# Hyena and short-convolution projections as seven block products per quad, on one Trainium2 core

## What is computed

```python
p = h @ lp['w_in']                       # h (2048, 1024)
yb = hyena_branch(p[..., B_OFF:C_OFF], lp, rows)    # 768 columns
yc = shortconv_branch(p[..., C_OFF:G_OFF], lp, rows) # 768 columns
# hyena: u = short_conv(pb, hy_conv_w, rows) + hy_conv_b
#        x0, x1, v = split(u, 3); z = x1 * v; y = x0 * (longconv(z) + z * hy_d_bias)
# shortconv: bg, cg, hx = split(pc, 3); y = bg * short_conv(cg * hx, sc_conv_w, rows)
# short_conv: three taps along each row of 64 tokens, zero at the row ends
```

## Time and profile before

| | us |
|---|---|
| runs of the kernel before, median (lowest to highest of 3) | 4469.63 (4462.31 to 4470.07) |
| the profiled execution | 4470.81 |
| its span in the profile | 4469.0 |
| projection stage, first to last matmul | 1412.43 to 1755.34 |
| gates' stage, first matmul | 2192.33 |

### The profile page before, as it was taken

One profiled execution on the slowest core, in us unless ns is written; L12 is line 12 of the kernel. 1 busy time (PEld: TensorE's weight loads), 2 busy tenths in 40 slices (PEclk: granted clock), 3 DMA queues, 4 the chain that ended last, 5 costly groups with the idle time before them and its releaser, 6 DMA issues. The chain is left out here.

```text
span 4469.0 us, 42953 instructions
## 1 busy us (share of the span) xinstructions
PE 3992.4 (89%) x15090; PEld 2435.5 (54%) x15090; DVE 1362.0 (30%) x2515; ACT 864.7 (19%) x1729; POOL 676.2 (15%) x536
## 2 busy tenths in 40 slices
PE   6999988989898998784499999989958999999994
PEld 2444445888886443242244444435537777777773
DVE  4433324666664121413322232212141111111112
ACT  4444441223222110020111111111100000000002
POOL 1122112333331000011100111112211000000000
PEclk9999998999999999897699999999969999999997
DMA  6333321222121101543311111124342455445544
GB/s 250 117 97 104 97 58 66 71 70 70 67 69 48 29 9 37 172 141 123 115 47 52 56 47 59 47 94 154 122 171 96 147 191 207 156 159 202 198 143 176
DMA packets 293866, 484.19 MB, mean 108 GB/s; under 512 B 20939, under 2 KB 171150, under 8 KB 293510
## 3 DMA queue, kind: packets, MB, share of 16 engines
q1 hardware_dynamic: 269618, 417.47, 27.0%
q0 software_dynamic: 12096, 43.86, 3.8%
q10 hardware_dynamic: 12053, 21.56, 1.5%
HBM read 372.05 MB, written 110.77 MB: 108 GB/s over the span
## 5 line engine op out<-in xcount | busy, mean ns | idle before, releaser
L2460 PE MATMUL bank<-xeT,wgu 128*128 128x256 f32 x3072 | 667.2, 380 | 9.9 <-PE bank L2474 9.8
L2460 PEld LDWEIGHTS bank<-xeT,wgu 128*128 128x128 f32 x3072 | 582.4, 190 | 100.9 <-issue 22.1
L627 PE MATMUL bank<-hT,wq 128*128 128x512 f32 x1024 | 450.1, 593 | 0.0
L1335 PE MATMUL bank<-hT,wh 128*128 128x512 f32 x768 | 336.5, 598 | 12.6 <-DMA wh<-in_w_in 9.6
L2474 PE MATMUL bank<-wd,hid_e 128*128 128x512 f32 x768 | 332.3, 592 | 1.5 <-DVE hid_e L2381 1.5
L627 PEld LDWEIGHTS bank<-hT,wq 128*128 128x128 f32 x1024 | 192.5, 190 | 224.9 <-issue 224.3
L1853 PE MATMUL bank<-hT,raw_w 128*128 128x512 f32 x576 | 261.1, 596 | 6.5 <-DMA raw_w<-in_w_in 6.5
L1335 PEld LDWEIGHTS bank<-hT,wh 128*128 128x128 f32 x768 | 145.6, 191 | 197.1 <-issue 197.1
L2111 PE MATMUL bank<-wo,mt 128*128 128x512 f32 x512 | 227.8, 599 | 15.7 <-DMA wo<-in_w_out 15.7
L2474 PEld LDWEIGHTS bank<-wd,hid_e 128*128 128x128 f32 x768 | 144.7, 190 | 177.9 <-issue 177.9
L2379 DVE TENSOR_TENSOR gm<-sgm,bank 128x256 f32<-128x256 f32 x96 | 40.4, 421 | 602.2 <-ACT sgm L2402 602.2
(11 more groups left out here) (351 smaller groups left out, 5223.7 us busy)
## 6 DMA issues: line engine op xcount, KB each, us to landing
wgu<-in_exp_w_gate SPq DMA_DIRECT2D x16, 3072.0 KB, 22.8
wgu<-in_exp_w_up SPq DMA_DIRECT2D x16, 3072.0 KB, 29.8
wd<-in_exp_w_down SPq DMA_DIRECT2D x16, 3072.0 KB, 13.5
ada<-in_ada_w SPq DMA_DIRECT2D x12, 2048.0 KB, 9.8
raw_w<-in_w_in SPq DMA_DIRECT2D x24, 1024.0 KB, 5.2
fa_d<-az ACTq DMA_DIRECT2D x48, 264.0 KB
sp_in<-fa_d SPq DMA_DIRECT2D x66, 192.0 KB, 4.1
kT<-kT_d SPq DMA_DIRECT2D x36, 256.0 KB, 2.8
```

What stands on the lines that cost most here:

```text
L627: last = pe.matmul(PS[g % 4][:, 0:width(n)], wq[:, kind, k, :], h_of(k, toff(n), width(n)), start=(k == 0), stop=(k == KD - 1))
L1335: last = pe.matmul(PS[u % 4][:, :], wh[:, kind, k, :], h_of(k, toff(n + 1), TW), start=(k == 0), stop=(k == KD - 1))
L2460: last = pe.matmul(PS[4 + f % 2][:, g * CAP:(g + 1) * CAP], wgu[:, b, g, k, f * P:(f + 1) * P], xeT[:, b, k, :], start=(k == 0), stop=(k = ...
```

## The change

The projection stage is rewritten with the gates' scheme. The unit is now a quad: one kind (256 columns, both halves) by 1024 tokens; 12 quads, 6 kinds for each half of the tokens. A quad is 7 products of 4 matmuls: p1, p5, c11, u2, c12, u3, c21. So 12 x 28 = 336 matmuls. Banks 0 and 1 take turns as X, banks 2 and 3 are Y and Z. VectorE gets four weight sums for each quad, four token sums for each half of the tokens, and three result sums for each quad. T3 has a tile of its own, since `hT` is read again by the gates' stage. Taps and products follow block by block (`middle` on ScalarE, `post` and `product_of` on VectorE). z is now made in `zT` itself, which gets its own memory; the GpSimd copy is gone. `yaT` is allocated later, and in the gates' stage T1 and T2 lie in the memory of `zT`, which is dead by then. The stage is unrolled, the store of z is issued by SyncE, and a load brings 1 MB for each quad. Nothing else is changed.

The core of the diff, indented less (the helpers `w`, `t`, `product`, `kept`, `s1` to `s4`, `t1`, `t2` and `t4` are as in the gates' stage):

```diff
@@ -1293,147 +1293,321 @@
-yaT = sbt(yst, "yaT", [P, HEADS, SEQ])
-zT = yaT[:, 0:2, :]
+zT = sbt(yst, "zT", [P, 2, SEQ])
...
+    T1, T2, T3, T4 = [sbt(st, n, [P, 4, TW]) for n in ("T1_h", "T2_h", "T3_h", "T4_h")]
+    p1s, p5s, u2s = [sbt(st, n, [P, TW]) for n in ("p1s_h", "p5s_h", "u2s_h")]
+    cb, cs = sbt(st, "cb_h", [P, 3, TW]), sbt(st, "cs", [P, 4, TW])
+    tmp, tm2, nat = [sbt(st, n, [P, 2, TW]) for n in ("tmp_h", "tm2", "nat_h")]
+    quads = [(p, kind) for p in range(2) for kind in range(6)]
+    NQ, QP = 12, 6
+    places = [(0, 0), (0, 1), (1, 1), (1, 0)]
+    conv_kinds = (0, 1, 2, 5)
+    convs = lambda q, i: sum(4 for v in quads[:q] if v[1] in conv_kinds) + i + 1
...
+    X, Y, Z = lambda q: PS[q % 2], PS[2], PS[3]
+    def at(v, q, i):
+        h, c = places[i]
+        return v[:, h, (2 * quads[q][0] + c) * TW:(2 * quads[q][0] + c + 1) * TW]
+    def summand(q, i):
+        kind = quads[q][1]
+        if kind == 3:
+            return at(ycT, q, i)
+        if kind == 4:
+            return cs[:, i, :]
+        return X(q)[:, :] if i == 3 else cb[:, i, :]
...
+            load_raw(0)
+            load_raw(1)
+            for q in range(1, NQ + 1):
+                p, kind = quads[q - 1]
+                if q + 1 < NQ:
+                    sp.wait_ge(c21_mm, q)
+                    load_raw(q + 1)
+                if kind == 3:
+                    for i, (h, c) in enumerate(places):
+                        sp.wait_ge(znat_ok, turned(p, i))
+                        sp.dma_start(z_d[(2 * p + c) * TW:(2 * p + c + 1) * TW, h * P:(h + 1) * P].rearrange("(j p) c -> p j c", p=P),
+                                     nat[:, i % 2, :].rearrange("p (j c) -> p j c", c=P)).then_inc(z_st[i % 2], 16)
+            for b in range(2):
+                sp.wait_ge(z_st[b], 64)
...
+            def turn(q, i):
+                p = quads[q][0]
+                pe.wait_ge(post_ok, convs(q - 1, i))
+                if turned(p, i) > 2:
+                    pe.wait_ge(znat_ok, turned(p, i) - 2)
                 for j in range(4):
+                    last = pe.transpose(PS[4 + i % 2][:, j * P:(j + 1) * P], at(zT, q, i)[:, j * P:(j + 1) * P], eye[:, :])
                 last.then_inc(z_tr, 1)
+            for q in range(NQ):
+                p, kind = quads[q]
+                pe.wait_ge(raw_in[q % 2], 16 * (q // 2 + 1))
+                if q >= 2:
+                    pe.wait_ge(x_free, q - 1)
+                product(X(q), w(q, 0, 0), t(p, 0, 0), True).then_inc(p1_mm, 1)
+                pe.wait_ge(s1_ok, q + 1)
+                pe.wait_ge(t1_ok, p + 1)
+                if q >= 1:
+                    pe.wait_ge(c12_ok, q)
+                product(Z, S1, T1, True).then_inc(p5_mm, 1)
+                if q >= 1:
+                    pe.wait_ge(c11_ok, q)
+                product(Y, w(q, 0, 1), t(p, 1, 0), True).then_inc(c11_mm, 1)
+                if kind == 3:
+                    turn(q, 0)
+                pe.wait_ge(s2_ok, q + 1)
+                pe.wait_ge(t2_ok, p + 1)
+                pe.wait_ge(p1s_ok, q + 1)
+                product(X(q), S2, T2, False).then_inc(u2_mm, 1)
+                if kind == 3:
+                    turn(q, 1)
+                pe.wait_ge(s4_ok, q + 1)
+                pe.wait_ge(p5s_ok, q + 1)
+                product(Z, S4, t(p, 1, 1), False).then_inc(c12_mm, 1)
+                if kind == 3:
+                    turn(q, 2)
+                pe.wait_ge(s3_ok, q + 1)
+                pe.wait_ge(t3_ok, p + 1)
+                pe.wait_ge(u2s_ok, q + 1)
+                product(X(q), w(q, 1, 0), T3, False).then_inc(u3_mm, 1)
+                if kind == 3:
+                    turn(q, 3)
+                pe.wait_ge(t4_ok, p + 1)
+                pe.wait_ge(c22_ok, q + 1)
+                product(X(q), w(q, 1, 1), T4, False).then_inc(c21_mm, 1)
...
+            for q in range(NQ):
+                if q >= 1:
+                    middle(q - 1, 3)
+                kept(p1s, X(q), p1_mm, c11_ok, p1s_ok, q)
+                kept(p5s, Z, p5_mm, c22_ok, p5s_ok, q)
+                middle(q, 0)
+                to_nat(q, 0)
+                kept(u2s, X(q), u2_mm, c12_ok, u2s_ok, q)
+                middle(q, 1)
+                to_nat(q, 1)
+                to_nat(q, 2)
+                middle(q, 2)
+                to_nat(q, 3)
+            middle(NQ - 1, 3)
...
+            def summed(q, i, bank, mm, other, other_ok, ok):
+                dve.wait_ge(mm, q + 1)
+                dve.wait_ge(other_ok, q + 1)
+                if q >= 1 and quads[q - 1][1] in conv_kinds:
+                    dve.wait_ge(post_ok, convs(q - 1, i))
+                dve.tensor_tensor(summand(q, i), bank[:, :], other[:, :], ALU.add).then_inc(ok, 1)
+            def product_of(q, i):
+                if quads[q][1] != 5:
+                    return
+                if i == 3:
+                    dve.wait_ge(c21_mm, q + 1)
+                else:
+                    dve.wait_ge((c11_ok, c12_ok, c22_ok)[i], q + 1)
+                if i < 2:
+                    dve.wait_ge(post_ok, convs(q - 3, 3))
+                else:
+                    dve.wait_ge(post_ok, convs(q, i - 2))
+                if i == 3:
+                    dve.wait_ge(x_free, q)
+                last = dve.tensor_tensor(tmp[:, i % 2, :], cs[:, i, :], summand(q, i), ALU.mult)
+                last.then_inc(prod_ok, 1)
+            def post(q, i):
+                p, kind = quads[q]
+                h, c = places[i]
+                if kind in (3, 4):
+                    if i == 3:
+                        dve.wait_ge(c21_mm, q + 1)
+                        dve.tensor_copy(summand(q, i), X(q)[:, :]).then_inc(x_free, 1)
+                    return
+                grid = lambda v: v.rearrange("p (r c) -> p r c", c=GRID_W)
+                if kind == 5:
+                    src, to, base, step = grid(tmp[:, i % 2, :]), grid(tm2[:, i % 2, :]), R_SCW + h, 2
+                else:
+                    src, to, base, step = grid(summand(q, i)), grid((at(x0T, q, i), at(zT, q, i), tmp[:, i % 2, :])[kind]), R_HYW + kind * 2 + h, 6
+                n = convs(q, i)
+                dve.wait_ge(mid_ok, n)
+                dve.scalar_tensor_tensor(to[:, :, 1:GRID_W], src[:, :, 0:GRID_W - 1], cols[:, base:base + 1], to[:, :, 1:GRID_W],
+                                         ALU.mult, ALU.add).then_inc(tap_ok, 1)
+                dve.wait_ge(tap_ok, 2 * n - 1)
+                last = dve.scalar_tensor_tensor(to[:, :, 0:GRID_W - 1], src[:, :, 1:GRID_W], cols[:, base + 2 * step:base + 2 * step + 1],
+                                                to[:, :, 0:GRID_W - 1], ALU.mult, ALU.add)
+                last.then_inc(tap_ok, 1)
+                dve.wait_ge(tap_ok, 2 * n)
+                if kind == 2:
+                    dve.tensor_tensor(at(zT, q, i), at(zT, q, i), tmp[:, i % 2, :], ALU.mult).then_inc(post_ok, 1)
+                elif kind == 5:
+                    dve.tensor_tensor(at(ycT, q, i), at(ycT, q, i), tm2[:, i % 2, :], ALU.mult).then_inc(post_ok, 1)
+                else:
+                    dve.sem_inc(post_ok, 1)
+                if i == 3:
+                    dve.sem_inc(x_free, 1)
...
+            def t3(p):
+                if p:
+                    dve.wait_ge(u3_mm, QP * p)
+                dve.tensor_tensor(T3[:, :, :], t(p, 1, 1), t(p, 0, 1), ALU.subtract).then_inc(t3_ok, 1)
...
+            for q in range(NQ + 1):
+                turn = q == QP - 1
+                if q >= 1:
+                    product_of(q - 1, 3)
+                    post(q - 1, 2)
+                if q % QP == 0 and q < NQ:
+                    t4(q // QP)
+                if q < NQ:
+                    summed(q, 0, Y, c11_mm, p1s, p1s_ok, c11_ok)
+                    product_of(q, 0)
+                if q >= 1:
+                    post(q - 1, 3)
+                if q == NQ:
+                    break
+                if q + 1 < NQ:
+                    s1(q + 1)
+                    s3(q + 1)
+                if q % QP == 0:
+                    t3(q // QP)
+                if turn:
+                    t1(1)
+                summed(q, 1, Z, c12_mm, u2s, u2s_ok, c12_ok)
+                product_of(q, 1)
+                post(q, 0)
+                if q + 1 < NQ:
+                    s2(q + 1)
+                if turn:
+                    t2(1)
+                summed(q, 2, X(q), u3_mm, p5s, p5s_ok, c22_ok)
+                product_of(q, 2)
+                if q + 1 < NQ:
+                    s4(q + 1)
+                post(q, 1)
...
+yaT = sbt(yst, "yaT", [P, HEADS, SEQ])
...
-    T1, T2, T4 = [sbt(st, n, [P, 4, TW]) for n in ("T1", "T2", "T4")]
+    T1, T2 = [zT[:, x, :].rearrange("p (k t) -> p k t", t=TW) for x in range(2)]
+    T4 = sbt(st, "T4", [P, 4, TW])
```

More of the change, by code:

```diff
@@ L1313, in _, with load_raw @@
                 def _(sp):
[L1314 to L1318, removed]
+                    def load_raw(q):
+                        c0 = B_OFF + quads[q][1] * HW
```

(27 more changed lines are left out.)

120 lines of the change are left out of this document (70 added, 50 removed).

## The result

| | before | after |
|---|---|---|
| median of 4 runs each (lowest to highest), us | 4466.83 (4462.31 to 4470.07) | 4436.52 (4432.9 to 4436.96) |
| span in the profile | 4469.0 | 4435.2 |
| projection stage, first to last matmul | 342.9 | 311.6 |

The changed kernel takes 0.993 of the time before, 95% interval 0.9915 to 0.9944: 30.3 us less between the medians. The forecast was 27.8 less, 4443.0, range 4430 to 4456. The absolute figure is 6.5 us too high: 4.0 of that is its base, the one profiled execution of 4470.8 us where the median of before is now 4466.8, and 2.5 is the difference.

A forecast was written before the change was run, and what follows sets the result against it. TensorE's passes laid end to end were taken to bound the projection stage. Stage 312.6 us against 342.9, 30.3 less; with 1.0 and 1.5 at the ends, 27.8 less: 4470.8 - 27.8 = 4443.0 us, range 4430 to 4456.

The forecast's parts named there:

- start at half clock: First passes of the projection stage run at half clock, costing 3.0 us more; this stays after the change.
- VectorE's tail, more: After the stage's last matmul VectorE has a product and two whole blocks, 5.4 us against 3.97: 1.5 us more.
- What bounds the kernel: Projection stage is TensorE's passes laid end to end, busy 339.0 of 342.9 us; a pass taken out shortens the program.
- The stop before c21: Between u3 and c21 TensorE waits for VectorE's sum: 1.12 us for each of 12 quads, 13.4 us.
- The lateness of VectorE: VectorE reaches its sum of u3 late in some quads, 3.2 us in quad 5: 3.8 us in all.
- The restart: After quad 5's stop of some 4 us, TensorE's clock restart costs between nothing and 3.0 us; 1.5 taken.
- The first load: At the stage's start, 1 MB instead of 512 KB: 5.05 us from issue to first matmul against 4.05, 1.0 more.
- The cover I named for the rest: Other new work in the stage (weight loads, ScalarE's copies, token sums, store of z) is hidden; a lost load cover costs 5.2 us.
- Rival 1: VectorE is one operation behind in each quad, doubling the gap before c21: 12.5 us more, 4455; chance 0.09.
- Rival 2: The chain of engines, not the passes, sets every quad: 34.6 us more, 4478, no change; chance 0.04.
- Rival 3: Short stops before c21 pull TensorE's clock down, grant 0.86: 46.9 us more, 4490, slower; chance 0.05.
- Rival 4: Passes go, but the gain is lost in the next stage, which waits for its own loads: 4470; chance 0.04.

The follow-up runs named there:

- eighth_product: Changed kernel plus an eighth product of 4 matmuls per quad between u3 and c21, into a bank nobody reads: stage 336.3 us, 4457.56 us in one run.
- t2_late: Changed kernel with token sum T2 of the second half behind VectorE's sum of u3 in quad 5: stage 307.8 us, 4435.20 us in one run.
- gap_3us: Changed kernel with one unread 128x2048 VectorE operation before the sum of u3 in each quad: stage 351.5 us, 4481.19 us in one run.
- after_again: Changed kernel, unchanged, profiled a second time: stage 311.6 us, 4436.28 us.
- fill_gap: Changed kernel with the next quad's first product p1 moved between u3 and c21: stage 300.6 us, median 4424.35 us, 0.9903 of before.
- before_again: Kernel before the change, unchanged, profiled a second time: stage 342.9 us, 4469.71 us.
- fill_t2_split: fill_gap plus T2 of the second half behind the sum of u3 and the first weight load as two of 512 KB: stage 299.0, median 4424.19 us.

## Why the prediction was right, point by point

| term | forecast | measured |
|---|---|---|
| 672 passes at 0.429 us | 288.3 | products 3.43 us apart throughout |
| start at half clock | 3.0 | 2.4 (1415.46 to 1421.31, less 3.43) |
| stop before c21, each quad | 1.12 | 1.12 in quad 0 (1435.04 to 1443.02 less two products) |
| lateness in quads 2, 8, 11, 5 | 0.1, 0.1, 0.4, 3.2 | 0, 0, 0.05, 2.9 |
| restart in quad 5 | 1.5 | 1.7 |
| stage | 312.6 | 311.6 |
| first load to first matmul, more | 1.0 | 1.5 (1409.90 to 1415.46 against 4.05) |
| VectorE's tail, more | 1.5 | 1.1 (1727.04 to 1732.08 against 3.97) |
| all of these | -27.8 | -28.7 |

**What bounds the kernel** held: eighth_product put the passes back, and the stage grew by them less the stops that they filled, to 0.1 us of what was expected. **The stop before c21** held to the hundredth, since the gates' first quad is the same pattern with the same operations.

**The lateness of VectorE** was the right mechanism in the right quad, and 0.9 us too large. The step that was mis-sized is the spacing of dependent operations: I took 0.87 us for a tap or product behind its input, the upper of two, and 0.84 for the product behind the sum that it reads. The last blocks of the changed stage show 0.77 throughout, and 0.72 from the sum to its product:

```profile
1722.54 0.68 DVE L1478 TENSOR_TENSOR cb_h<-bank,p5s_h 128x512 f32<-128x512 f32 x1
1723.26 0.69 DVE L1494 TENSOR_TENSOR tmp_h<-cs,cb_h 128x512 f32<-128x512 f32 x1
1723.87 0.73 DVE L1512 SCALAR_TENSOR_TENSOR tm<-tmp_h,cols,tm 128x504 f32<-128x504 f32 x1
...
1724.64 0.74 DVE L1515 SCALAR_TENSOR_TENSOR tm<-tmp_h,cols,tm 128x504 f32<-128x504 f32 x1
1725.41 0.69 DVE L1522 TENSOR_TENSOR ycT<-ycT,tm 128x512 f32<-128x512 f32 x1
```

The shorter tail has the same reason: two blocks of VectorE at 0.77 us a step.

**The restart** was a guess in the middle of 0 to 3.0 us, and that it came out near 1.7 is luck. t2_late showed that its cause is the long stop. The reading behind the lower bound was wrong. I took the row with 2.94 us of idle in the earlier trace rows for a stop that left the clock full, since the next pair of passes took 1.07 us. The rows behind it in the same trace say otherwise:

```profile
1800.97 1.91 PE L1472 MATMUL bank<-hb,fw 128*66 128x512 f32 x2
1802.67 1.06 PE L1474 MATMUL bank<-zb,fw 128*66 128x256 f32 x2
1803.53 1.28 PE L1472 MATMUL bank<-hb,fw 128*66 128x512 f32 x2
```

At full clock these pairs take 1.02 and 0.59 us. The clock fell within 1.5 us after the work had begun again, and the granted clock from 1801 to 1803 us is 0.50. From 1799.46 to the end of the slow pairs at 1804.64 it took 5.18 us where five pairs at full clock take 3.44 (three at 0.86, two at 0.43): 1.7 us, which is what quad 5 paid. The expectation for gap_3us rests on the same misreading.

**The first load** was mis-sized by 0.5 us. The price came from one load in the gates' stage, 5.05 us; here it was 5.56, 5.47 in after_again (1408.14 to 1413.61) and 5.35 in fill_gap (1405.04 to 1410.39). The gates' own load took 5.37 us in before_again (2185.84 to 2191.21) and 5.59 in after (2153.91 to 2159.50), so 5.05 was a short one.

**The cover I named for the rest** was thinner than I wrote. I said that the store of z is issued behind a load already issued. It is issued behind SyncE's wait for c21 of the same quad, ScalarE's third copy to `nat_h` waits for it, and the copy of p1 stands behind that:

```profile
1519.97 0.37 SPq L1348 DMA_DIRECT2D raw_h<-in_w_in  x1
1520.39 8.14 SPq L1360 DMA_DIRECT2D z_d<-nat_h  x4
...
1526.80 1.33 ACT L1454 ACTIVATE nat_h<-bank 128x512 f32<-128x512 f32 x2 [18.02 <-DMA z_d<-nat_h]
1528.03 0.59 ACT L1426 ACTIVATE p1s_h<-bank 128x512 f32<-128x512 f32 x1
...
1530.08 3.60 PE L1370 MATMUL bank<-T_h,S_h 128*128 128x512 f32 x8
```

p1 is copied by 1528.62, u2 starts at 1530.08: 1.5 us of margin were left. Nothing was lost in the changed kernel, and fill_gap, which brings u2 forward by one product, paid 3.8 us.

**The rivals.** Rival 1, a doubled stop, did not happen; quads 0 to 2 all show 0.88 us. Rival 2 did not, as only quad 5 was late. Rival 3 did not, but one of the two arguments against it was false: the 2.94 us of idle in the earlier trace rows did bring the clock down, and stops of 2.0 us did in five of nine quads. What carried the argument was the row with 0.88 us in the earlier trace rows. Had each stop been 3.1 us instead of 0.9, the change would have made the stage 8.6 us longer than before. Rival 4 did not happen: TensorE's idle time in front of the next stage grew from 11.14 to 11.94 us, and the rest of the gain arrived.

**The rest of the difference.** The two profiled spans differ by 33.8 us, 5.1 more than the terms above explain, and the stretch between the stages is 5.3 us shorter in them; smaller shifts elsewhere cancel (the last store in front of the stage is issued 1.8 us later in after, 1404.23 and 1406.06). The medians differ by 30.3. So of the 2.5 us by which the forecast missed them, 0.9 is in its own terms; the rest lies in stretches that it left at nothing and that move by several us between kernels with the same code there, so that they cost it no more is luck.

## What to carry to other kernels

A block scheme that saves products also shortens the chain through one accumulator: look for the product that adds to a bank right after another engine must read it, and put an independent product there, which took 11 us off the stage here by itself, and 17 us together with T2 behind the sum, the first load in halves and the store of z issued earlier. Price such a stop from a place in the same kernel where its usual filling is missing, as in the first turn of a loop. When you read whether a stop costs the clock, read on for several rows behind it, or ask for the granted clock: the first pair behind it can still be fast. And before moving work forward, read the waits of the engines that cost nothing now: an 18 us wait on ScalarE was free in one order and cost 2 us a time in the next.

## What the runs showed of the hardware

The clock's answer to a stop is not fixed by the stop's length. In the projection stage stops of up to 1.57 us never brought it down, nor did the four of 1.82 to 1.97 us in front of u2 in fill_gap and fill_t2_split. Stops of 2.0 us did in five of nine quads, 3.1 us in six of nine, 3.7 us and more in all six profiles that had one in quad 5. Each fall behind a stop of 2.0 to 3.1 us cost the next product 1.4 to 1.7 us (5.21 us instead of 3.50 in most), 2.9 us in one. A single stop of such a length proves neither.

An independent VectorE operation of 1024 elements in front of the sum made the stop 1.13 us longer, one of 2048 elements 2.20 us, exactly in all the quads where VectorE was free.
